# One-hot tiles of a gate scatter: all on VectorE in 16 bits, eight tokens interleaved

## The reference

```python
q = (hf @ wq).reshape(T, PEER_HEADS, 2, PEER_DKEY // 2)
sc = jnp.einsum('thpd,pnd->thpn', q, subkeys, preferred_element_type=jnp.float32)
top_v, top_i = lax.top_k(sc, PEER_TOPK)
...
best_v, best_j = lax.top_k(cand_v, PEER_TOPK)
ids = jnp.take_along_axis(cand_id, best_j, axis=-1)      # i1 * 128 + i2
gates = jax.nn.softmax(best_v, axis=-1)
...
a = jnp.einsum('td,ted->te', xb, u_tab[ids])
w = gb * jax.nn.gelu(a, approximate=False)
y = jnp.einsum('te,ted->td', w, v_tab[ids])
```

## Time and profile before

| | |
|---|---|
| median of 3 runs | 1294.67 us |
| profiled execution, its span | 1295.06 us, 1292.9 us |
| TensorE busy, weight loads busy | 1254.3 us (97%), 1138.5 us (88%) |
| VectorE busy | 981.9 us (76%) |
| ScalarE busy | 759.6 us (59%) |
| POOL busy | 390.4 us (30%) |
| DMA | 248.15 MB, mean 192 GB/s |

### The profile page before, as it was taken

The page is one execution under the profiler, slowest core; times in us unless marked ns, Lnnn a source line. Parts: engine busy times, 40 slices in busy tenths (PEclk is TensorE's granted clock), DMA queues, the critical chain, the costliest instruction groups (busy, mean ns, idle before and its releaser), DMA issues.

```text
span 1292.9 us, 26236 instructions
## 1 busy us (share of the span) xinstructions
PE 1254.3 (97%) x8596; PEld 1138.5 (88%) x8596; DVE 981.9 (76%) x1851; ACT 759.6 (59%) x1293; POOL 390.4 (30%) x254
## 2 busy tenths in 40 slices
PE   7989999999999989999999999999999999999997
PEld 7989999899999989999999888888888888888885
DVE  6999988897987767996999755556666666666666
ACT  6434445556766555558999644545555555555554
POOL 1179912225150147788888200000000000000000
PEclk9999999999999989999999999999999999999999
DMA  9978776453676245554434555556656566656662
GB/s 373 343 232 261 252 251 225 156 176 113 231 245 213 85 163 165 176 179 148 132 131 131 156 187 193 182 191 218 219 183 190 182 192 191 186 183 186 195 189 71
DMA packets 69344, 248.15 MB, mean 192 GB/s; under 512 B 7968, under 2 KB 8352, under 8 KB 68512
## 3 DMA queue, kind: packets, MB, share of 16 engines
q1 hardware_dynamic: 59920, 213.04, 51.1%
q10 hardware_dynamic: 9360, 34.27, 8.0%
HBM read 244.66 MB, written 2.62 MB: 191 GB/s over the span
## 4 chain that ended last, share of the span: by engine, by line
PE 61%; DVE 7%; ACT 5%; issue 2%; POOL 1%; DMA 0%; DVEq 0%; POOLq 0%; ACTq 0%
PE ps L2500 26%; PE ps L1931 11%; PE ps L2511 10%; PE ps L2513 5%; DVE O L1640 2%; DVE O L1631 2%; ACT WH L506 2%; PE ps L2339 1%; PE ps L2102 1%; DVE A L1617 1%; ACT A L912 1%; ACT O2b L906 1%; POOL tmp L1870 1%; PE ps L2121 1%; PE ps L2428 1%
## 5 line engine op out<-in xcount | busy, mean ns | idle before, releaser
L1025 DVE TENSOR_TENSOR WL<-raw,WH 128x1024 fp32r<-128x1024 f32 x320 | 408.5, 1282 | 86.0 <-ACT WH L506 81.8
L506 ACT ACTIVATE WH<-raw 128x1024 fp32r<-128x1024 f32 x392 | 411.4, 1053 | 64.5 <-PE ps L1931 30.7
L1931 PE MATMUL ps<-X,WH 128*128 128x256 f32 x1888 | 350.9, 287 | 1.4 <-DVE WL L1025 1.2
L1931 PEld LDWEIGHTS ps<-X,WH 128*128 128x128 f32 x1888 | 294.7, 192 | 2.2 <-DVE WL L1025 1.4
L1931 PE MATMUL ps<-X,WL 128*128 128x256 f32 x944 | 267.6, 283 | 0.0
L2511 PE MATMUL ps<-X,WH 128*128 128x512 f32 x576 | 205.5, 397 | 0.0
L2500 PE MATMUL ps<-WH,wvL 128*128 128x512 f32 x496 | 195.5, 394 | 0.0
L2500 PE MATMUL ps<-WH,wvH 128*128 128x512 f32 x496 | 195.3, 394 | 0.1
L2500 PE MATMUL ps<-WL,wvH 128*128 128x512 f32 x496 | 195.3, 394 | 0.0
L1897 POOL TENSOR_TENSOR WL<-raw,WH 128x1024 fp32r<-128x1024 f32 x72 | 173.6, 2415 | 59.1 <-ACT WH L506 59.0
L1931 PEld LDWEIGHTS ps<-X,WL 128*128 128x128 f32 x944 | 181.3, 192 | 0.0
(11 more groups left out here) (358 smaller groups left out, 2284.7 us busy)
## 6 DMA issues: line engine op xcount, KB each, us to landing
raw<-stream SPq DMA_DIRECT2D x392, 512.0 KB, 3.6
ada<-adaT ACTq DMA_DIRECT2D x47, 512.0 KB, 4.1
bias<-att_bias ACTq DMA_DIRECT2D x8, 512.0 KB, 4.7
x<-xT ACTq DMA_DIRECT2D x2, 512.0 KB, 5.8
raw<-stream SPq DMA_DIRECT2D x4, 256.0 KB, 6.0
ws<-wsT SPq DMA_DIRECT2D x1, 1024.0 KB, 8.4
lng<-rows SPq DMA_DIRECT2D x1, 1024.0 KB, 8.1
lnb<-rows SPq DMA_DIRECT2D x1, 1024.0 KB, 8.6
```

The source lines that it names most:

```text
L506: act.activation(WH[:, slot, :], raw[:, slot, :], ACT.Copy).then_inc(h_done, 1)
L1025: dve.tensor_tensor(WL[:, slot, :], raw[:, slot, :], WH[:, slot, :].bitcast(F32), ALU.subtract).then_inc(l_done, 1)
L1931: mm = pe.matmul(out_ap, a(kc), b(kc), start=(first and kc == 0 and i == 0), stop=(last and kc == KC - 1 and i == 2))
```

## The change

1. The one-hots of a round are four tiles of [128, 128, 8] in fp16: `hot_eq` (entry equals i1), `hot_high` and `hot_low` (times the high and the low half of the gate), and `hot_second` (entry equals i2). The eight tokens are innermost, so the one-hot of one token is every eighth element of the tile. VectorE makes all of them, with four operations of 1024 elements a round; the work of POOL and ScalarE on one-hots is gone. There is one set, not two halves.
2. One operand of the comparisons is `iota8`, the numbers 1 to 128, each eight times in a row, made once by ScalarE behind the exponential. The lists of i1 and i2 are kept plus one.
3. The four lists (i1, gate high, gate low, i2), 256 fp16 values each, are gathered in `lists` in SBUF and written to bank 2 of PSUM as 512 32-bit words, by a shift by zero. The comparisons and products read them there as fp16.
4. The transposes of the lists come one up tile sooner on TensorE; ScalarE's conversion of the gate moves one tile sooner too.
5. TensorE waits once a round, for `hot_ready`.

```diff
+        hot_high, hot_low, hot_second, hot_eq, iota8 = (
+            nc.alloc_sbuf_tensor_at(name, [P, NK, 8], F16, offset=base_hot + i * NK * 16)
+            for i, name in enumerate(("hot_high", "hot_low", "hot_second", "hot_eq", "iota8")))
...
+        def of_eight(k, e):
+
+            row = ps[:, 2, :].bitcast(F16)
+            return row[:, k * T + 8 * e:k * T + 8 * e + 8].unsqueeze(1).broadcast_to([P, NK, 8])
...
@@ ScalarE
+            act.activation(iota8[:, :, :], iota.unsqueeze(2).broadcast_to([P, NK, 8]), ACT.Identity,
+                           bias=ones[:, 0:1]).then_inc(iota_ready, 1)
+            for j in range(TOP - 8, TOP - 2):
                 early_step(j)
+            act.wait_ge(lt_mm, 1)
+            act.activation(lists[:, 1, :], gate_l, ACT.Copy, scale=GATE_SCALE).then_inc(gate_high, 1)
+            early_step(TOP - 2)
             hi(C_U + 3 + TOP - 1)
-            act.wait_ge(lt_mm, 1)
-            act.activation(gate_h[:, :, 1], gate_l, ACT.Copy, scale=GATE_SCALE).then_inc(gate_high, 1)
-            act.activation(tmp[2][:, :], i2_l, ACT.Copy).then_inc(lt_ready, 1)
...
-                if e + 1 < ROUNDS:
-                    hot_second(e + 1)
                 gates_out(e)
...
@@ VectorE
             dve.wait_ge(lt_mm, 1)
+            dve.tensor_scalar(lists[:, 3, :], i2_l, 1.0, None, ALU.add)
             dve.wait_ge(gate_high, 1)
+            dve.tensor_scalar(lists[:, 0, :], i1_l, 1.0, None, ALU.add)
+            dve.scalar_tensor_tensor(out=lists[:, 2, :], in0=gate_l, scalar=GATE_SCALE, in1=lists[:, 1, :],
                                      op0=ALU.mult, op1=ALU.subtract).then_inc(gate_low, 1)
             dve.wait_ge(gate_low, 1)
+            dve.tensor_scalar(ps[:, 2, :].bitcast(U32), lists[:, :, :].rearrange("p k t -> p (k t)").bitcast(U32), 0, None,
+                              ALU.logical_shift_right).then_inc(gate_packed, 1)
...
+            def hots(e):
+                if e >= 1:
+                    dve.wait_ge(hot_ready, e)
+                dve.tensor_tensor(hot_eq[:, :, :], iota8[:, :, :], of_eight(0, e), ALU.is_equal).then_inc(eq_ready, 1)
                 if e >= 2:
                     product_round(e - 2)
+                if e >= 1:
+                    dve.wait_ge(gate_mm, 2 * e)
+                dve.tensor_tensor(hot_second[:, :, :], iota8[:, :, :], of_eight(3, e), ALU.is_equal)
+                dve.wait_ge(eq_ready, e + 1)
+                dve.tensor_tensor(hot_high[:, :, :], hot_eq[:, :, :], of_eight(1, e), ALU.mult)
+                dve.tensor_tensor(hot_low[:, :, :], hot_eq[:, :, :], of_eight(2, e), ALU.mult).then_inc(hot_ready, 1)
...
@@ POOL
-            distance(0)
-            pool_low(C_U + TOP + 2)
-            distance(1)
-            for e in range(ROUNDS):
-                pool_low(C_U + TOP + 3 + e)
-                if e + 2 < ROUNDS:
-                    distance(e + 2)
+            for e in range(ROUNDS + 1):
+                pool_low(C_U + TOP + 2 + e)
@@ TensorE
-            for j in range(TOP - 4, TOP - 1):
+            for j in range(TOP - 4, TOP - 2):
                 early_up(j)
             pe.wait_ge(lists_ready, 1)
...
             mm.then_inc(lt_mm, 1)
-            early_up(TOP - 1)
+            for j in range(TOP - 2, TOP):
+                early_up(j)
...
+                pe.wait_ge(hot_ready, e + 1)
                 for n in range(8):
                     half, k = n // 4, n % 4
-                    if k == 0:
-                        pe.wait_ge(hot2_ready[half], e + 1)
-                        pe.wait_ge(hot_ready, 2 * e + half + 1)
+                    for first, hot in ((True, hot_high), (False, hot_low)):
+                        mm = pe.matmul(ps[:, gate_bank(e) + half, k * P:(k + 1) * P], hot[:, :, n], hot_second[:, :, n],
+                                       start=first, stop=not first)
```

More of the change, by code:

```diff
@@ L161, in two_block_kernel @@
                           for name, t in (("firstH", tmp[0]), ("firstL", tmp[1])))
[L163 to L167, removed]
+        hot_high, hot_low, hot_second, hot_eq, iota8 = (
+            nc.alloc_sbuf_tensor_at(name, [P, NK, 8], F16, offset=base_hot + i * NK * 16)
+            for i, name in enumerate(("hot_high", "hot_low", "hot_second", "hot_eq", "iota8")))
+        lists = nc.alloc_sbuf_tensor_at("lists", [P, 4, T], F16, offset=base_hot)
         assert base_hot + 20 * NK * 4 <= base
@@ L317, in two_block_kernel @@
         tr_mm, spill_done = sem("tr_mm"), sem("spill_done")
-        lists_ready, lt_mm, lt_ready, exp_in, exp_ready = (
-            sem("lists_ready"), sem("lt_mm"), sem("lt_ready"), sem("exp_in"), sem("exp_ready"))
-        hot2_ready = [sem(f"hot2_ready{i}") for i in range(2)]
+        lists_ready, lt_mm, iota_ready, exp_in, exp_ready = (
+            sem("lists_ready"), sem("lt_mm"), sem("iota_ready"), sem("exp_in"), sem("exp_ready"))
         gm_ready, prod_ready, eq_ready = sem("gm_ready"), sem("prod_ready"), sem("eq_ready")
-        dist_ready, dist2_ready = sem("dist_ready"), sem("dist2_ready")
         hot_ready, gate_mm, gate_out = sem("hot_ready"), sem("gate_mm"), sem("gate_out")
@@ L441, in fours @@
                     step(j, g)
-        iota4 = iota.unsqueeze(1).broadcast_to([P, 4, NK])
-        def of_four(row, e, half):
-            return row[:, 8 * e + 4 * half:8 * e + 4 * half + 4].unsqueeze(2).broadcast_to([P, 4, NK])
+        def of_eight(k, e):
+            row = ps[:, 2, :].bitcast(F16)
+            return row[:, k * T + 8 * e:k * T + 8 * e + 8].unsqueeze(1).broadcast_to([P, NK, 8])
         def bout_bank(n):
@@ L922, in gelu_round @@
                 ins.then_inc(gelu_ready, 1)
-            hot_second(0)
             early_gelu(TOP - 1)
@@ L1603, in _ @@
             dve.wait_ge(lt_mm, 1)
+            dve.tensor_scalar(lists[:, 3, :], i2_l, 1.0, None, ALU.add)
             dve.wait_ge(gate_high, 1)
-            dve.scalar_tensor_tensor(out=gate_h[:, :, 0], in0=gate_l, scalar=GATE_SCALE, in1=gate_h[:, :, 1],
+            dve.tensor_scalar(lists[:, 0, :], i1_l, 1.0, None, ALU.add)
+            dve.scalar_tensor_tensor(out=lists[:, 2, :], in0=gate_l, scalar=GATE_SCALE, in1=lists[:, 1, :],
                                      op0=ALU.mult, op1=ALU.subtract).then_inc(gate_low, 1)
             dve.wait_ge(gate_low, 1)
-            dve.tensor_copy(gate_l, gate_w[:, :]).then_inc(gate_packed, 1)
-            dve.wait_ge(lt_ready, 1)
+            dve.tensor_scalar(ps[:, 2, :].bitcast(U32), lists[:, :, :].rearrange("p k t -> p (k t)").bitcast(U32), 0, None,
+                              ALU.logical_shift_right).then_inc(gate_packed, 1)
+            dve.wait_ge(iota_ready, 1)
+            dve.wait_ge(gate_packed, 1)
             def gated_round(e):
@@ L1625, in product_round @@
                 dve.tensor_tensor(A[:, j, 0:n], A[:, j, 0:n], ps[:, j % 2, 0:n], ALU.mult).then_inc(prod_ready, 1)
-            def hot_first(e, half):
+            def hots(e):
                 if e >= 1:
[L1630 to L1640, removed]
-            for e in range(ROUNDS):
[L1643 to L1646, removed]
+                    dve.wait_ge(hot_ready, e)
+                dve.tensor_tensor(hot_eq[:, :, :], iota8[:, :, :], of_eight(0, e), ALU.is_equal).then_inc(eq_ready, 1)
                 if e >= 2:
                     product_round(e - 2)
-                hot_gated(e, 1)
+                if e >= 1:
[4 more added lines that the diff above has]
+                dve.tensor_tensor(hot_low[:, :, :], hot_eq[:, :, :], of_eight(2, e), ALU.mult).then_inc(hot_ready, 1)
+            for e in range(ROUNDS):
+                hots(e)
                 if e >= 1:
@@ L2464, in _ @@
                     pe.wait_ge(gate_out, e - 1)
+                pe.wait_ge(hot_ready, e + 1)
                 for n in range(8):
                     half, k = n // 4, n % 4
-                    if k == 0:
-                        pe.wait_ge(hot2_ready[half], e + 1)
-                        pe.wait_ge(hot_ready, 2 * e + half + 1)
-                    for part in (1, 0):
-                        mm = pe.matmul(ps[:, gate_bank(e) + half, k * P:(k + 1) * P], O1[:, n, :].bitcast(F16).rearrange("p (i x) -> p i x", x=2)[:, :, part],
-                                       (O2a, O2b[:, e % 2])[half][:, k, :], start=(part == 1), stop=(part == 0))
+                    for first, hot in ((True, hot_high), (False, hot_low)):
+                        mm = pe.matmul(ps[:, gate_bank(e) + half, k * P:(k + 1) * P], hot[:, :, n], hot_second[:, :, n],
+                                       start=first, stop=not first)
                     if k == 3:
```

7 lines of the change are left out of this document (removed).

## The result

The changed kernel takes 1380.38 us, the median of four runs (1378.46 to 1381.96); the kernel before took 1294.12 beside it. The ratio is 1.0664, 95% interval 1.0650 to 1.0677: 6.6% slower, where I had forecast 0.7% faster. The profiled execution took 1378.46 us (span 1376.7), 83.4 more than before's 1295.06.

The account below looks back on a forecast made before the run. VectorE and ScalarE were taken to bound the one-hot stage, TensorE afterwards. First gates at 592.0 plus 32 rounds of 3.84 end at 714.9 against 724.36, 9.5 us less: 1285.2 us, range 1282.5 to 1319.

Parts of the forecast that it names:

- TensorE's count "and cost": Gate matmuls in the one-hot stage: same count, each still 0.054 us despite 16-byte steps, so rounds of 3.84 us.
- rival A's second case: TensorE's strided gate matmuls cost 0.215 us each, 6.42 a round, 1368 us in all; chance 0.07.
- my sum: The forecast's total, with 16-byte operand steps free on TensorE: 9.5 us less than before, 1285.2 us.
- The second half of A's bound: Upper bound for a strided gate matmul, from ScalarE's strided write at 1.68 ns an element: 0.215 us for 128.
- VectorE at two elements a cycle: Each one-hot operation of 1024 elements takes 0.60 us start to start, so VectorE's round is 3.35 to 3.74.
- rival B: VectorE stays at one element a cycle in the one-hot stage: 5.5 us a round, 1337 us; chance 0.12.
- ScalarE and POOL relieved: In the one-hot stage ScalarE falls from 4.12 to 2.8 us a round and POOL far under a round; neither bounds.
- One set of one-hots costs nothing: VectorE's wait each round for TensorE's gates is hidden by the tile: 1.9 of 2.98 us, costed at nothing.
- Rival C: Waits and ScalarE's gating copy leave rounds at 3.95 to 4.05 us: 1289 to 1292 us; chance 0.13.
- The start: Ahead of the first gates: sooner transposes remove a 2.2 us loss, `iota8` adds a 0.4 stall; first gates at 592.0.
- What follows the stage: After the last tile, remaining gating, product and split stay hidden behind TensorE's work, so the stage's saving is kept.

Follow-up runs that it names:

- e5: Changed kernel with a dense moving operand and the loaded operand's step growing from 1 to 8 elements, gates incorrect: 1284.26 us.
- e10: Changed kernel with a dense moving operand and the loaded operand read from a constant tile at steps of 8 to 48 elements, gates incorrect: 1289.6 us.
- e4: Changed kernel with a dense loaded operand and the moving operand's step growing from 1 to 8 elements, gates incorrect: 1325.9 us.
- e3: Changed kernel with both operands of the gate matmuls reading adjacent elements, gates incorrect: 1284.37 us.
- e2: Changed kernel with only the loaded operand dense, the moving one keeping its 16-byte step, gates incorrect: 1379.31 us.
- e6: Changed kernel with four tokens innermost instead of eight, so operands step by 8 bytes, correct gates: 1315.57 us.
- e11: e7 with the i2 one-hots made tokens outermost, so the moving operand is dense and the list value repeats at step zero: 1288.16 us.
- e7: Changed kernel with two tokens innermost instead of eight, so operands step by 4 bytes, correct gates: 1285.03 us.
- e8: e7 with the list transposes and the gate's conversion put back one tile later: 1288.08 us.
- e9: Changed kernel with a dense loaded operand and the moving one read from a constant tile at steps of 8 to 48 elements, gates incorrect: 1400.78 us.

## Why the prediction was wrong, point by point

**TensorE's count "and cost": the step that failed.** I wrote of the strided gate matmul "I take 0.054, as the row nearest in engine and type", with 0.215 as the upper bound. Measured in the same way, by weight loads, it took 0.221 (3.53 / 16), and 0.235 from start to start, just over that upper bound; 1380.38 is above rival A's second case, 1368, which had 0.07. The error was in the choice of the row. It showed an operand that is *loaded* with a step of 4 bytes; the moving operand of those gate matmuls was contiguous. (The sentence "No strided matmul operand stands in the trace" left this out: one did, on the loaded side.) e5 and e10 show that the loaded operand is nearly indifferent to its step, e4 that the moving one pays for every element of step beyond 4 bytes, up to 16. I carried a row from one operand to the other.

The size: a round is 6.65 instead of 3.84, which over 32 rounds makes 89.9 us, and four dips of the clock add 4.3; together 94.2, which is 217.1 - 122.9. With both operands dense (e3) the round is 3.83.

The page "SBUF — State Buffer" of the Trainium skill gives two rules in its paragraph on cachelines, and my sum agreed with the one that calls eight bf16 a free stride. The runs bear out neither: eight elements cost 0.212 by weight loads (e2), and two hits on a line, which the page's other sentence asks for, still cost 0.111 (e6).

**The second half of A's bound.** The 0.215 came from ScalarE's strided write, 1.68 ns an element. The moving operand's 3.63 / 16 in e2 is 1.77 ns an element. That the two are so near may be chance: ScalarE's write stepped by 1 KB, and e4 shows that for TensorE the price follows the step. But a bound that is itself a measured strided price deserved more than 0.07.

**VectorE at two elements a cycle: right.** 680 ns, 0.60 from start to start, as taken; rival B is out. The page "VectorE: DVE Perf Modes" of the Trainium skill, section "The perf-mode tier table", would have given a list operand in PSUM single rate; the row of 680 ns is against it. Section 5.1 of the Trainium skill's "Vector Engine (DVE) Microarchitecture Reference" stands, and e11's 1.22 us is its reverse side, a source with inner step zero.

**ScalarE and POOL relieved: right.** Within the stage the chains of e3 and e7 hold TensorE alone.

**One set of one-hots costs nothing: right**, by e3: rounds of 3.83 from 641.26 to 645.09. Rival C, which had rounds of 3.95 to 4.05, did not come.

**The start: right in what it gives, with one size off.** The gates are ready 1.06 ahead of TensorE (589.92 to 590.98; 0.9 forecast). `iota8` cost 0.50 at 572.97, where I had 0.4 at 573.6; e7, whose row of numbers is a quarter as long, has no such pause. The gates began at 590.98, not 592.0, because TensorE was already about 1.2 ahead of the trace of before when it came to that pause (572.47, where before's tile starts at 573.64). e8 puts the sooner transposes at 3.05, above the 2.2 that I took.

**What follows the stage: right.** 568.6 against 568.5.

**The clock: not in the prediction.** Four tiles at 1.2 GHz behind strided gates, 4.3 us in all. Of the loss it is a twentieth. The gates themselves do not pay for it.

What stays open: why the price rises again at 80 and 96 bytes, and what brings the dips of the clock. Within the stage they came at steps of 7 elements and more in e4, in e2, e9 and the changed kernel, and in none of the other experiments; that is where they occur, not a cause.

## What to carry to other kernels

A layout has two readers, and an estimate needs a row for each: before tokens, heads or channels are interleaved for VectorE, look for a row of TensorE with that very step on that very operand. If there is none, interleave only as far as the moving operand's step stays at 4 bytes: that cost 0.055 instead of 0.054 a matmul here, and a run of two gave VectorE all of its double rate. Where the choice between two bounds decides the sign, and no row lies near, the upper bound deserves real weight.

## What the runs showed of the hardware that I had not expected

- A 128-column fp16 matmul costs 0.060 us at a moving step of 2 elements, about 0.0275 more for each further element, and 0.228 at 8 (the chain of e4). It stays near that up to 32 elements and rises again at 40 and 48 (4.27 / 16 = 0.27 and 5.12 / 16 = 0.32, e9). The loaded operand's step adds 0.016 at most (e5, e10).
- At a moving step of 8 elements this price does not depend on the granted clock: the gate matmuls follow each other by 0.23 us at 1.00 and at 0.50.
- The granted clock fell to 0.50 inside a stretch in which TensorE had no idle time, near the end of sixteen matmuls of a wide moving step, and stayed there until 657.0 in the round shown.
- VectorE works on fp16 at nearly twice the rate of fp32 (680 ns against 1222 for 1024 elements) with one input in PSUM, also when the other input repeats a run of two, but not when the list is repeated with an inner step of zero (1.22 us, e11).
